# Two weight pieces per transfer: 16 KB per partition in one DMA, slots freed in pairs

## The reference

```python
xb = h_pad[tok]                                   # the tokens of one expert
gu = xb @ w_gu[e] + b_gu[e]                       # 1024 x 2048 weights
glu = jnp.minimum(gu[:, :D_EXPERT], SWIGLU_LIMIT)
lin = jnp.clip(gu[:, D_EXPERT:], -SWIGLU_LIMIT, SWIGLU_LIMIT)
act = glu * jax.nn.sigmoid(SWIGLU_ALPHA * glu) * (lin + 1.0)
return (act @ w_down[e] + b_down[e]) * g[:, None] # 1024 x 1024 weights
```

## Time and profile before

| what | value |
|---|---|
| median of three runs | 1449.99 us |
| profiled execution | 1450.44 us |
| its span | 1448.7 us |
| TensorE busy (modelled) | 1369.2 us, 95% |
| VectorE busy | 1261.1 us, 87% |
| ScalarE busy | 1117.4 us, 77% |
| weight pieces | 384 loads of 1 MB |

### The profile page before, as it was taken

The page is one execution under the profiler, slowest core; times in us unless marked ns, Lnnn a source line. Parts: engine busy times, 40 slices in busy tenths (PEclk is TensorE's granted clock), DMA queues, the critical chain, the costliest instruction groups (busy, mean ns, idle before and its releaser), DMA issues. The chain is left out here.

```text
span 1448.7 us, 18694 instructions
## 1 busy us (share of the span) xinstructions
PE 1369.2 (95%) x6693; PEld 1112.4 (77%) x6696; DVE 1261.1 (87%) x1314; ACT 1117.4 (77%) x1221; POOL 220.0 (15%) x138
## 2 busy tenths in 40 slices
PE   6999878999999999999999999999999999999995
PEld 5887766786788878778777788787787787787884
DVE  5799778548899899999999899989999999998994
ACT  5666554455788898988988788988889888888783
POOL 1222000011111111211202011111111111030100
PEclk9999979999999999999999999999999999999998
DMA  5522011158999999999999999999999999999991
GB/s 152 148 71 73 30 59 45 45 193 307 332 382 376 371 379 398 405 389 396 395 401 386 395 374 401 406 388 393 387 389 397 381 391 379 400 391 385 378 391 30
DMA packets 85926, 448.52 MB, mean 310 GB/s; under 512 B 18496, under 2 KB 23616, under 8 KB 36608
## 3 DMA queue, kind: packets, MB, share of 16 engines
q1 hardware_dynamic: 73424, 428.32, 75.0%
q0 software_dynamic: 9792, 18.90, 5.4%
q10 hardware_dynamic: 2608, 0.01, 0.1%
HBM read 440.89 MB, written 23.07 MB: 320 GB/s over the span
## 5 line engine op out<-in xcount | busy, mean ns | idle before, releaser
L840 DVE TENSOR_TENSOR whl<-wraw,whl 128x2048 fp32r<-128x2048 f32 x384 | 864.3, 2286 | 70.8 <-ACT whl L835 68.6
L835 ACT ACTIVATE whl<-wraw 128x2048 fp32r<-128x2048 f32 x384 | 728.5, 1917 | 143.3 <-PE ps L2163 95.6
L2163 PE MATMUL ps<-whl,xT 128*128 128x512 f32 x2768 | 660.5, 394 | 8.4 <-DVE whl L840 3.9
L2163 PEld LDWEIGHTS ps<-whl,xT 128*128 128x128 f32 x2768 | 514.0, 188 | 124.8 <-DVE whl L840 14.8
L2163 PE MATMUL ps<-whl,aT 128*128 128x512 f32 x1312 | 314.1, 396 | 14.2 <-DVE whl L840 14.2
L2163 PEld LDWEIGHTS ps<-whl,aT 128*128 128x128 f32 x1312 | 245.2, 189 | 68.5 <-DVE whl L840 18.4
L1029 POOL DMA_INDIRECT out_dram<-ysb,idx x32 | 86.0, 2688 | 623.2 <-ACT ysb L1344 623.2
L1020 POOL DMA_INDIRECT xg<-h_rows,idx x32 | 84.7, 2648 | 258.8 <-DVE idx L1794 253.7
L1906 PE MATMUL ps<-W,HT 128*128 128x512 f32 (+1 forms) x184 | 72.1, 392 | 5.4 <-DVE W L612 4.4
L1908 PE MATMUL ps<-W,HT 128*128 128x512 f32 (+1 forms) x184 | 68.9, 375 | 0.0
L1907 PE MATMUL ps<-W,HT 128*128 128x512 f32 (+1 forms) x184 | 68.8, 374 | 0.0
(11 more groups left out here) (296 smaller groups left out, 1400.8 us busy)
## 6 DMA issues: line engine op xcount, KB each, us to landing
wraw<-in_w_gu_dram SPq DMA_DIRECT2D x256, 1024.0 KB, 15.8
wraw<-in_w_down_dram SPq DMA_DIRECT2D x128, 1024.0 KB, 14.5
WR<-in_w_in_dram SPq DMA_DIRECT2D x20, 512.0 KB, 3.7
WR<-in_w_o_dram SPq DMA_DIRECT2D x8, 512.0 KB, 3.7
xs<-in_x_dram SPq DMA_DIRECT2D x4, 512.0 KB, 7.7
WR<-in_x_dram SPq DMA_DIRECT2D x4, 512.0 KB, 3.8
out_dram<-WR SPq DMA_DIRECT2D x4, 512.0 KB, 3.3
h_rows<-WR SPq DMA_DIRECT2D x4, 512.0 KB, 2.6
```

The lines of the kernel that those rows point to most:

```text
L835: act.activation(whl[:, n % HL, 0, :], wraw[n % RAW], ACT.Copy).then_inc(chunk_hi, 1)
L840: eng.tensor_tensor(whl[:, n % HL, 1, :], wraw[n % RAW], whl[:, n % HL, 0, :].bitcast(F32), ALU.subtract).then_inc(chunk_lo, 1)
L2163: ins = pe.matmul(bank, a[x_][j], w[:, b, j, 512 * q:512 * q + 512], start=c == NG and j == 0 and n == 0, stop=last and j == nj - 1 and n ...
```

## The change

Slots are joined in pairs: four tiles `wpair` of 128 x 2 x 2048, and `wraw[s]` is a view of one half of one. One load brings pieces c and c+1 (c even): 2 MB, 16 KB per partition. `landed` has four semaphores, one for each pair; both pieces of a pair wait for the same count. The load waits until both pieces that held the pair have been split. For `w_gu` the two rows 256 q + 2 p and 256 q + 2 p + 1 lie behind each other on partition p, so that the 16 KB are contiguous in HBM; the transposes of the tokens take every second column to match. For `w_down` four rows are taken together where two were, and each piece holds the same rows as before. All sizes and counts of the splits and of the products stay.

```diff
-        wraw = [place(f"wraw{s}", [P, 2048], F32, offset=base + 8192 * s if s < 6 else o_qb + 66560 + 8192 * (s - 6))
-                for s in range(RAW)]
+        wpair = [place(f"wpair{s}", [P, 2, 2048], F32, offset=base + 16384 * s if s < 3 else o_qb + 66560)
+                 for s in range(RAW // 2)]
+        wraw = [wpair[s // 2][:, s % 2, :] for s in range(RAW)]
@@
-        landed = [sem(f"landed{s}") for s in range(RAW)]
+        landed = [sem(f"landed{s}") for s in range(RAW // 2)]
@@
-                return w_gu[0, at_, c * P:(c + 1) * P, :]
-            return w_down[0, at_].rearrange("(p q j) n -> p q j n", q=ND, j=2)[:, c - NG]
+                return w_gu[0, at_, c * P:(c + 2) * P, :].rearrange("(p j) n -> p j n", j=2)
+            return w_down[0, at_].rearrange("(p u m) n -> p u m n", u=ND // 2, m=4)[:, (c - NG) // 2]
@@
-            w = wraw[n % RAW]
-            after(eng, chunk_lo, PER_ROUND * r + n - RAW + 1)
-            eng.dma_start(w if c < NG else w.rearrange("p (j n) -> p j n", j=2),
+            w = wpair[n // 2 % (RAW // 2)]
+            after(eng, chunk_lo, PER_ROUND * r + n - RAW + 2)
+            eng.dma_start(w if c < NG else w.rearrange("p s (j n) -> p (s j) n", j=2),
                           chunk_src(e, c, at_)) \
-               .then_inc(landed[n % RAW], 16)
+               .then_inc(landed[n // 2 % (RAW // 2)], 16)
@@
-            act.wait_ge(landed[n % RAW], 16 * (PER_ROUND // RAW * r + n // RAW + 1))
+            act.wait_ge(landed[n // 2 % (RAW // 2)], 16 * (PER_ROUND // RAW * r + n // RAW + 1))
@@
-                    for c in range(6):
+                    for c in range(0, 6, 2):
                         load_chunk(sp, 0, 0, c)
@@
-            for c in range(6, NG):
+            for c in range(6, NG, 2):
                 load_chunk(sp, 0, 0, c)
@@
-                    if not is0(r) or chunk_no(e, c) >= RAW:
+                    if c % 2 == 0 and (not is0(r) or chunk_no(e, c) >= RAW):
                         load_chunk(sp, r, e, c, ids_at.get(e))
@@
+                by_row = xg[j % 2].rearrange("s (q p u) -> s q u p", q=KD // 2, u=2)
                 for b in range(2):
                     for k in range(4):
                         ins = pe.transpose(ps[:, TP + b, k * P:(k + 1) * P],
-                                           xg[j % 2][:, (4 * b + k) * P:(4 * b + k + 1) * P], ident)
+                                           by_row[:, 2 * b + k // 2, k % 2, :], ident)
```

## The result

The changed kernel takes 1455.95 us (median of 20 runs, 1452.83 to 1462.47) where the kernel before took 1450.80 beside it (20 runs, 1447.59 to 1453.71). The ratio is 1.0041, with a 95% interval of 1.0032 to 1.0049: slower by 0.41%, and outside the range given above. The profiled execution of the changed kernel took 1460.41 us, its span 1458.7: 4.5 us over its median, and 10.0 us longer than the span of the kernel before. Of these 10.0 us, 2.0 arise before the first weight piece is asked for (at 313.0 us against 311.0). So the stage of the experts is compared by its own marks.

A forecast was written before the change was run, and what follows sets the result against it. Engines bound the kernel first, weight transfers after 700 us. Packets' 11.6 us saved less 1.2 us lost made -10.4 us, so the profiled 1450.44 us became 1440.0, 1439.5 as median; range 1435 to 1452 us.

The forecast's parts named there:

- Freeing in pairs: SyncE's load waits for the second subtraction; first half asked 2.29 to 4.6 us later, DMA still has work ahead: costs nothing.
- 10 us of reserve: Before 700 us a landed piece is in its slot 14.4 us, where the splits need 4.2 us.
- The landing of the first half: First piece waits 2.48 us for the second, taken from the reserve once: net about zero, 1.2 us lost for scatters.
- the 11 ns a packet: Weight loads: joining two 8 KB packets into one of 16 KB saves this, 0.53 us an expert, 11.6 us over 22.
- The second reading: 8 KB packets at 315 ns in a 3 us stretch leave 7 ns saved per packet, 0.34 us an expert.
- The queue isn't short of requests, the DMA engines are its limit: After 700 us, issue to landing of 16.4 us means several pieces are always queued ahead.
- Transposes, gathers, scatters: Token transposes of every second column cost zero; gathers and scatters may land later, but no instruction waits for a gather's landing.
- B: Weight transfers: 16 KB split again or bytes alone limit, so no packet gain; 1450 to 1453.7 us, likely 1451; chance 0.12.
- D: Weight loads: part of 2.48 us belongs to each transfer, so halving transfers saves up to the ceiling: 1435.5 us; chance 0.06.
- the ceiling: Last 22 experts: transfers cost 0.66 us each, so pieces at any speed end the stage at most 14.5 us earlier.
- E: TensorE: the transposes' longer weight loads are on the path, +12.3 us, so 1452 us; chance 0.06.
- C: SyncE's wait before a pair: queue runs dry, DMA engines stand still 2.3 us each time; 1455 us; chance 0.10.

The follow-up runs named there:

- the fifth pair slot: Changed kernel with gate-up bias products replaced, plus one more 16 KB pair slot from the 25th piece on: 1451.18 us, 0.9957 of the same with four pair slots.
- the ninth single one: Kernel before with one more single 8 KB slot from the 25th piece on, in space dead by then: 1447.53 us, 0.9983 of the kernel before.
- the ring of six: Kernel before with six single slots for raw pieces instead of eight: 1456.55 us, 1.0053 of the kernel before.
- both waits at 8 KB: Kernel before with requests and landings both waiting in pairs, still single 1 MB transfers in 8 KB packets: 1462.39 us, 1.0081 of the kernel before.
- its control with single pieces: Kernel before with the products adding gate-up biases taking the tokens instead of the biases: 1452.69 us, 1.0022 of the kernel before.
- the run with the rows alone: Kernel before with gate-up rows interleaved and transposes over every second column, pieces, requests and landings single: 1451.54 us, 1.0005 of the kernel before.
- the control with three split slots: Kernel before with three slots for split pieces instead of four, eight raw slots kept: 1520.99 us, 1.0494 of the kernel before.

## Why the prediction was wrong

**The step that failed: "Freeing in pairs ... Cost: nothing".** It asked one thing, whether the queue could fall quite empty, and found 12.2 - 4.6 = 7.6 us against a need of 7.2. That much held: in the changed kernel the landings from 700 to 1400 us came after

```profile
DMA to landing us min/median/max: 10.7/13.6/17.6
```

at the least 10.7 us. Still the engines were idle 1.4% more. Sixteen engines needn't all stand still for time to be lost. Which engine had nothing left, and when, the trace's packets don't say, so the way from later requests to idle engines is argued, not shown; that more slots fill the engines again is seen with the fifth pair slot (98.5% instead of 97.8) and, less, with the ninth single one (99.2 instead of 99.0). The freeing alone, with 8 KB packets, measured 0.57%, 8.3 us (5.1 to 11.3), where the sum had nothing.

**The reserve was worked out for the landing, not for the request.** The prediction had 10 us of reserve in the stage that the engines limit, and took one piece time from it. The late request takes another: a pair is asked for when its second half is free, 2.74 us after its first. The landings from 425 to 518 us, of the changed kernel, of the kernel with a ninth slot and of that with a fifth pair slot:

```profile
DMA to landing us min/median/max: 7.8/9.7/11.9
```

```profile
DMA to landing us min/median/max: 5.4/8.1/11.2
```

```profile
DMA to landing us min/median/max: 8.5/11.0/13.0
```

In the prediction's own way: the loop of eight pieces is 21.9 us, the pair lands 9.7 after its request, and it needs 2.74 + 4.2 = 6.9 us in the slot. That leaves 5.3 us, not 7.5. For the ninth slot 24.7 - 8.1 - 4.2 = 12.4, for the fifth pair 27.4 - 11.0 - 6.9 = 9.5, and for the kernel before 10.2. For the ring of six it is 16.4 - 7.4 - 4.2 = 4.8. These estimates go with the early waits: 15.5 us of waits for pieces from 515 to 680 us at a reserve of 4.8, 7.3 at 5.3, none at 9.5, 10.2 and 12.4. They say nothing of the last 22 experts, where the profiled changed kernel lost most.

**The landing of the first half: "net about zero", paid once.** The prediction put 1.2 us down for it. It measured 0.39%, 5.6 us, by itself (interval 3.5 to 7.8). So it isn't paid once out of a reserve. An argument for why, which no run tests: after 700 us there are only some 2 us of reserve, and if every scatter between two pieces spends it again, what was taken from it is missed each time.

**The packets: right in kind, half the size.** 11.6 us were put down, 0.53 us an expert. 0.27 us an expert came, 5.9 us, by the shares of queue 1; the changed kernel against both waits at 8 KB gives 5.8, with its wide interval. The mis-sized term is the 11 ns a packet, the step that "should save the same 12 ns again". Packet by packet, from 700 to 1390 us, the median one of 16 KB took 611 ns and that of 8 KB 309: 7 ns for each joined packet, where the step from 4 to 8 KB, at a median of 160 ns, is 11. The second reading of the same paragraph, 7 ns, would have given 7.5 us. The 4 KB packets of the earlier trace rows are stores to `out_dram` and `h_rows`, not loads, which the prediction didn't say; the 4 KB loads of the first 60 us have a median of 161 ns, so this didn't move the sum. The Trainium skill's page Perfetto Trace Analysis, section "DMA Optimizations", says that larger DMAs use the memory's bandwidth better, and next to it that smaller ones may start sooner where the DMA engines are mostly idle. The trace agrees with the first by 0.86%; of the second no run here shows anything, since the engines are 99% busy.

**"The queue isn't short of requests, the DMA engines are its limit"** was nearly so: 99.0% busy. But a ninth slot still won 0.17%, so even the kernel before was short of requests now and then.

**Transposes, gathers, scatters:** right in the sum, which had nothing for them. The weight loads became longer than either kind in the trace of before, 206 ns, and cost nothing. The gathers now wait 48.9 us for scatters, a wait that the kernel before hasn't got; the kernel with five pair slots has 48.1 us of it and is as fast as its control with single pieces.

**The rivals.** B (no gain from the packet) fell: 0.86% less engine time a byte. D fell: the joint transfer brought nothing like the 14.5 us of the ceiling. (What the prediction quotes for D from the Trainium skill's page DMA: Bandwidth & Descriptors, section "Anatomy of one DMA", is stated there for DMAs that GpSimd issues; these loads are SyncE's.) E fell by the run with the rows alone. C was the nearest, in place and sign: the load's wait for a second slot. Its form was wrong: its signs, landings of 7 to 8 us and slices of the DMA under 9, weren't seen (13.6 us in the median, no slice under 9 from 700 to 1390 us). Engines were partly idle, not the whole queue dry, so its 1455 us come near the measured time by another sum, by luck.

## What to carry to other kernels

Before transfers are joined, work out what the ring of slots loses: a joined slot is asked for when its last part is free and is usable when its last part has landed, so each joining costs lead at both ends. Compare this with the reserve in the stage that comes before the one limited by transfers. The order of the requests and of the landings can be tried by itself, with the small transfers, before anything is joined. And count busy shares to a tenth of a per cent: at 99% busy, a per cent of idle engines outweighs some nanoseconds a packet. If there is space to be had, even for part of the time, one more slot of the small kind can be the better use of it.

## What was not expected of the hardware

Packets of the same 8 KB don't cost the same engine time in every kernel: 39.74 us a MB in the kernel before, 39.78 in the ring of six (93.2% for 258.65 MB), 40.12 when they went out in twos, and 41.39 in the control with three split slots (91.6% for 244.32 MB), whose requests go out singly. So the order of requests isn't the only thing that changes it. The median packet took 309 ns in each of the four; what differs is a small number of long ones (from 700 to 1390 us 95 of 1200 ns or more in the kernel before, 206 freed in pairs). Why is open: the trace doesn't tell which engine a packet is on. A weight load of TensorE from every second column took 206 ns, from every eighth 188 and from neighbouring ones 140.
